# The first block's projection stage in another order: head 0's attention among the convolution's chunks, mean and variance behind the last chunk

## The reference

```python
q, k, v, u = split(proj)                # 4 heads, q and k with two parts of 64, v with 128
q, k = apply_rope(q), apply_rope(k)
a = softmax(q1 k1^T, causal) - lam * softmax(q2 k2^T, causal)
attn = rmsnorm(a @ v) * sub_g * (1 - lam_init)
z = (u_a + b_a) * sigmoid(u_gate + b_gate)          # 512 channels, as 4 chunks of 128
z = depthwise causal convolution, 31 taps, + bias
conv = silu(layer_norm(z over channels))
h = h + concat(attn, conv) @ w_out
h = h + (silu(gate) * up) @ w_down                  # gate, up = rmsnorm(h) @ w_gate_up
```

## Time and profile before

| | us |
|---|---|
| median of 3 runs (1738.6 to 1741.92) | 1740.06 |
| the profiled execution | 1738.21 |
| its span, first to last instruction | 1736.6 |
| TensorE busy in the span | 1661.4 (96%) |
| VectorE busy | 971.8 (56%) |
| ScalarE busy | 688.5 (40%) |
| GpSimd busy | 62.0 (4%) |

### The profile page before, as it was taken

The page is one execution under the profiler, slowest core; times in us unless marked ns, Lnnn a source line. Parts: engine busy times, 40 slices in busy tenths (PEclk is TensorE's granted clock), DMA queues, the critical chain, the costliest instruction groups (busy, mean ns, idle before and its releaser), DMA issues.

```text
span 1736.6 us, 26907 instructions
## 1 busy us (share of the span) xinstructions
PE 1661.4 (96%) x10642; PEld 1309.8 (75%) x10642; DVE 971.8 (56%) x1705; ACT 688.5 (40%) x1225; POOL 62.0 (4%) x48
## 2 busy tenths in 40 slices
PE   8889999998989999999999999999999999999997
PEld 6678999986789999878898989897544454545453
DVE  6967777769677777576756697665121212121212
ACT  2155434321554444465543577632222232323222
POOL 0100000001000000005110000000000000000000
PEclk9999999999999999999999999998999999999999
DMA  6222666752226667532402333336899999999993
GB/s 278 97 74 101 228 230 242 262 198 97 95 100 219 236 242 290 200 122 96 141 25 98 146 132 135 142 139 269 327 423 422 421 422 422 422 422 422 423 422 137
DMA packets 63963, 404.66 MB, mean 233 GB/s; under 512 B 12928, under 2 KB 14464, under 8 KB 15232
## 3 DMA queue, kind: packets, MB, share of 16 engines
q1 hardware_dynamic: 63440, 401.86, 59.3%
q10 hardware_dynamic: 432, 1.51, 0.2%
HBM read 401.91 MB, written 1.44 MB: 232 GB/s over the span
## 4 chain that ended last, share of the span: by engine, by line
PE 76%; DVE 16%; ACT 5%; issue 1%; DMA 0%; SPq 0%; DVEq 0%; ACTq 0%
PE ps L1441 20%; PE ps L847 19%; PE ps L988 10%; DVE big L2234 5%; PE ps L1414 4%; PE ps L1431 4%; PE ps L672 2%; DVE inv L2487 2%; DVE wlo L2298 2%; ACT whi L1634 2%; PE ps L1321 1%; DVE wlo L2665 1%; PE ps L1353 1%; PE ps L1382 1%; ACT wb L1842 1%
## 5 line engine op out<-in xcount | busy, mean ns | idle before, releaser
L2298 DVE TENSOR_TENSOR wlo<-ring,whi 128x2048 fp32r<-128x2048 f32 x76 | 174.2, 2292 | 90.3 <-ACT whi L1634 90.0
L847 PE MATMUL ps<-hg_hi,whi 128*128 128x272 f32 (+1 forms) x672 | 191.3, 285 | 2.4 <-DVE big L2430 2.4
L847 PE MATMUL ps<-hg_hi,wlo 128*128 128x272 f32 (+1 forms) x672 | 191.4, 285 | 0.0
L847 PE MATMUL ps<-hn_lo,whi 128*128 128x272 f32 (+1 forms) x672 | 190.8, 284 | 0.0
L1441 PE MATMUL ps<-big 128*64 128x512 f32 x816 | 181.8, 594 | 0.7 <-ACT big L2122 0.7
L1441 PE MATMUL ps<-ring,big 128*64 128x512 f32 x816 | 181.7, 594 | 0.0
L1634 ACT ACTIVATE whi<-ring 128x2048 fp32r<-128x2048 f32 x76 | 144.9, 1907 | 70.4 <-PE ps L847 51.8
L2951 DVE TENSOR_TENSOR ylo<-ps,yhi 128x512 fp32r<-128x512 f32 x68 | 47.0, 692 | 172.2 <-ACT yhi L2145 137.3
L672 PE MATMUL ps<-hn,ring 128*128 128x272 f32 x576 | 138.3, 398 | 0.0
L1441 PEld LDWEIGHTS ps<-big 128*64 128x64 f32 x816 | 57.5, 137 | 106.9 <-issue 106.6
L1441 PEld LDWEIGHTS ps<-ring,big 128*64 128x64 f32 x816 | 57.1, 137 | 107.2 <-issue 106.8
(11 more groups left out here) (456 smaller groups left out, 3585.9 us busy)
## 6 DMA issues: line engine op xcount, KB each, us to landing
ring<-in_stream SPq DMA_DIRECT2D x277, 1024.0 KB, 5.4
big<-in_stream SPq DMA_DIRECT2D x102, 1024.0 KB, 10.6
h<-in_xT SPq DMA_DIRECT2D x1, 1088.0 KB, 5.1
out_xT<-h SPq DMA_DIRECT2D x1, 1024.0 KB, 4.7
big<-in_consts ACTq DMA_DIRECT2D x1, 896.0 KB, 4.7
cst<-in_consts SPq DMA_DIRECT2D x1, 576.0 KB, 6.1
cs<-in_c_rows SPq DMA_DIRECT2D x1, 512.0 KB, 17.6
big<-in_consts ACTq DMA_DIRECT2D x1, 326.5 KB, 3.5
```

The source lines that it names most:

```text
L847: m = mm(out, a[:, at_:at_ + P], b[:, kept], start=first and i == 0, stop=last and i == 2)
L2298: v.tensor_tensor(wlo[j][:, :], ring[:, j, :], whi[d % 3][:, :], ALU.subtract).then_inc(wlo_ready, 1)
```

## The change

The first slot is now `qk0`, so the raw product gives q0 and k0 and the pair of VectorE evictions goes into `raw`. Head 0 (units 0 and 1) is rotated, scored and weighed among the convolution's chunks; the taps are spread over a longer list of other VectorE work; `mu` and `var` move from behind k2 and q3 to behind V3. The tail's `weigh` waits for all values. `DC + 2` counts of `raw_step` become `DC`. Lines of the order before, which stand in the kernel above, are cut.

```diff
-IN_ORDER = "glu0 glu1 glu2 glu3 qk0 v01 qk1 qk2 qk3 v23".split()
+IN_ORDER = "qk0 glu0 glu1 v01 glu2 glu3 qk1 qk2 qk3 v23".split()
-WORK = "v0 g0 v1 g1 v2 g2 v3 g3 q0 k0 rq0 V0 rk0 V1 t0 q1 t1 k1 rq1 q2 rk1 k2 mu rq2 q3 var rk2 k3 rq3 V2 rk3 s0 s1 V3 t2 t3".split()
+WORK = ("q0 k0 v0 rq0 g0 rk0 v1 g1 V0 V1 t0 t1 v2 g2 v3 g3 q1 k1 rq1 q2 rk1 k2 rq2 q3 rk2 k3 rq3 V2 rk3 s1 V3 mu "
+        "s0 var t2 t3").split()
@@ TensorE @@
-                        if slot_name == "glu1" and n == 0:
+                        if slot_name == "glu0" and n == 0:
                             W(pe, "hn_ready", k + 1, l)
...
-                    bank = ps[:, BANK[("v0", "g0")[n]], :]
+                    bank = ps[:, BANK[("q0", "k0")[n]], :]
...
                         if UNITS[u] == "tail":
+                            W(pe, "v_ready", 8, l)
...
+                chunk("glu0", 0, "v0")
+                rotate("q0")
+                chunk("glu0", 1, "g0")
+                rotate("k0")
+                chunk("glu1", 0, "v1")
+                scores(0)
+                chunk("glu1", 1, "g1")
+                scores(1)
+                chunk("v01", 0, "V0")
+                turn_probs(0)
+                chunk("v01", 1, "V1")
+                turn_v(0)
+                turn_probs(1)
+                turn_v(1)
+                chunk("glu2", 0, "v2")
+                weigh(0)
+                chunk("glu2", 1, "g2")
+                weigh(1)
                 chunk("glu3", 0, "v3")
                 chunk("glu3", 1, "g3")
...
                 chunk("qk1", 0, "q1")
                 chunk("qk1", 1, "k1")
                 rotate("q1")
                 chunk("qk2", 0, "q2")
                 rotate("k1")
                 chunk("qk2", 1, "k2")
+                scores(2)
+                rotate("q2")
+                chunk("qk3", 0, "q3")
+                scores(3)
+                rotate("k2")
+                turn_probs(2)
+                chunk("qk3", 1, "k3")
+                turn_probs(3)
+                weigh(2)
+                rotate("q3")
+                scores(4)
+                chunk("v23", 0, "V2")
+                weigh(3)
+                rotate("k3")
+                scores(5)
+                turn_probs(4)
+                chunk("v23", 1, "V3")
+                tail_scores()
+                turn_v(2)
+                turn_probs(5)
+                weigh(4)
                 W(pe, "conv_ready", 1, l)
                 bank = take("mu")
...
+                scores(7)
+                weigh(5)
+                turn_probs(6)
+                turn_v(3)
+                scores(8)
                 W(pe, "ln_step", 3, l)
                 bank = take("var")
...
                 weigh(6)
                 turn_probs(7)
+                weigh(7)
+                turn_probs(8)
...
                 add_out(0, conv_part, True, False, [0])
-                weigh(7)
-                turn_probs(8)
                 weigh(8)
@@ ScalarE @@
+                gate_out(0)
+                gate_out(1)
+                exps(0)
                 value_out(0)
+                exps(1)
+                probs_out(0)
                 value_out(1)
                 turned_value_out(0)
+                probs_out(1)
+                turned_value_out(1)
+                head_out(0)
+                gate_out(2)
+                head_out(1)
+                gate_out(3)
                 raw_out("q1")
                 raw_out("k1")
                 raw_out("q2")
                 raw_out("k2")
                 exps(2)
...
+                exps(4)
+                value_out(2)
+                head_out(3)
+                exps(5)
+                probs_out(4)
+                high_weights(0)
+                value_out(3)
+                exps(6)
+                turned_value_out(2)
+                probs_out(5)
+                head_out(4)
+                exps(7)
+                W(act, "ln_step", 2, l)
+                f(lsq[:, :, :], xc[:, :, :], ACT.Square).then_inc(ln_step, 1)
+                head_out(5)
+                probs_out(6)
+                turned_value_out(3)
+                exps(8)
                 W(act, "ln_step", 4, l)
                 f(root[:, 1, :], work("var", L), ACT.Sqrt, bias=small[:, 60:61], scale=1.0 / (CC * P)).then_inc(ln_step, 1)
+                head_out(6)
+                probs_out(7)
+                head_out(7)
...
+                probs_out(8)
+                W(act, "conv_out", CC, l)
+                f(xhi[:, 4:8, kept], cat[:, 4:8, kept], ACT.Copy).then_inc(xhi_ready, 1)
+                head_out(8)
+                high_weights(1)
+                W(act, "o_squared", 10, l)
+                f(small[:, 49:58], small[:, 40:49], ACT.Sqrt, scale=1.0 / P).then_inc(o_squared, 1)
                 if l == 0:
                     act.wait_ge(ada_loaded, 16)
                     f(cs[:, :], cs[:, :], ACT.Silu).then_inc(cs_ready, 1)
@@ VectorE @@
-                    if c == 0:
-                        dve.wait_ge(slot_done, l * PE_SLOTS + 1)
-                        v.tensor_tensor(sgl[:, 0, :], ps[:, BANK["g0"], 0:L], inv[:, 0, :], ALU.mult).then_inc(raw_step, 1)
-                        v.tensor_tensor(xc[:, 0, :], ps[:, BANK["v0"], 0:L], inv[:, 0, :], ALU.mult).then_inc(raw_step, 1)
...
+                for name in ("q0", "k0"):
...
+                    v.tensor_tensor(raw[:, j, :], ps[:, BANK[name], 0:L], inv[:, 0, :], ALU.mult).then_inc(raw_ready, 1)
                 W(dve, "lam_step", 3, l)
...
+                with_sin("q0")
+                with_sin("k0")
+                glu(0)
+                convolve(8, (0,))
+                maxima(0)
+                convolve(4, (0,))
                 glu(1)
+                difference(0)
+                maxima(1)
+                convolve(8, (0, 1))
+                difference(1)
+                convolve(26, (0, 1))
                 glu(2)
+                convolve(18, (0, 1, 2))
                 glu(3)
                 convolve(12, (0, 1, 2, 3))
+                with_sin("q1")
+                convolve(6, (0, 1, 2, 3))
+                with_sin("k1")
+                convolve(4, (0, 1, 2, 3))
+                maxima(2)
+                with_sin("q2")
+                difference(2)
+                maxima(3)
+                convolve(4, (0, 1, 2, 3))
+                with_sin("k2")
+                difference(3)
+                convolve(6, (0, 1, 2, 3))
+                with_sin("q3")
+                maxima(4)
                 convolve(8, (0, 1, 2, 3))
+                difference(4)
+                with_sin("k3")
+                maxima(5)
+                convolve(8, (0, 1, 2, 3))
+                difference(5)
                 convolve(sum(TAPS - t for t in taps.values()), (0, 1, 2, 3))
+                maxima(6)
+                maxima(7)
+                difference(6)
                 W(dve, "ln_step", 1, l)
...
+                difference(7)
+                maxima(8)
+                low_weights(0)
                 W(dve, "ln_step", 5, l)
                 link(v.reciprocal(inv[:, 1, :], root[:, 1, :]))
...
+                difference(8)
                 W(dve, "xhi_ready", 1, l)
...
+                low_weights(1)
                 W(dve, "o_squared", 11, l)
                 link(v.reciprocal(small[:, 49:58], small[:, 49:58]))
```

More of the change, by code:

```diff
@@ L810, in _ @@
                 m.then_inc(ln_step, 1)
[L811 to L827, removed]
-                weigh(4)
-                scores(7)
-                turn_v(3)
-                weigh(5)
-                turn_probs(6)
-                scores(8)
                 weigh(6)
                 turn_probs(7)
+                weigh(7)
+                turn_probs(8)
                 def both_parts(d):
@@ L1634, in high_weights @@
                     f(whi[d % 3][:, :], ring[:, s % RING, :], ACT.Copy).then_inc(whi_ready, 1)
-                for c in range(3):
-                    gate_out(c)
-                gate_out(3)
-                raw_out("q0")
-                raw_out("k0")
+                gate_out(0)
+                gate_out(1)
+                exps(0)
                 value_out(0)
+                exps(1)
+                probs_out(0)
                 value_out(1)
                 turned_value_out(0)
-                exps(0)
+                probs_out(1)
[4 more added lines that the diff above has]
+                gate_out(3)
                 raw_out("q1")
-                turned_value_out(1)
-                exps(1)
                 raw_out("k1")
-                probs_out(0)
                 raw_out("q2")
-                probs_out(1)
-                head_out(0)
                 raw_out("k2")
-                W(act, "ln_step", 2, l)
-                f(lsq[:, :, :], xc[:, :, :], ACT.Square).then_inc(ln_step, 1)
                 exps(2)
-                head_out(1)
                 raw_out("q3")
@@ L1661, in _ @@
                 probs_out(2)
+                raw_out("k3")
+                probs_out(3)
+                head_out(2)
+                exps(4)
```

(35 more changed lines are left out.)

75 lines of the change are left out of this document (9 added, 66 removed).

## The result

The changed kernel takes **1768.15 us** (median of four: 1764.17, 1767.8, 1768.51, 1768.8) against 1739.67 of the kernel before (four runs): a ratio of 1.0159, 95% interval 1.0143 to 1.0175. It is slower by 28 us; 1761 in 1750 to 1770 was forecast. The profiled execution is the quickest of the four: 1764.17, a span of 1762.5, 25.9 longer than before's.

What follows compares the result with a forecast made beforehand. TensorE was taken as bound, with some 17 us idle per layer to win, and VectorE's taps as the reason for lateness. Layer 0's +8.7 and 1.4 and layer 1's +11.0 gave +21: 1759 profiled, 1761 median, range 1750 to 1770.

Steps and rivals of the forecast that it cites:

- C + 34: First finish matmul in layer 0: 34 us behind the last convolution tap (C), after a chain of queued steps.
- Part 1: Head of the stage: VectorE waits 2.8 and 2.7 us, chunk v1 stalls 2.2, taps start at 31.3, not 24.0.
- rival (d): Exposed table loads pay the skill page's drain, three ScalarE steps each 1.4 us later: +8, 1769 us; chance 0.02.
- Parts 2 and 3: Middle through last tap: 76.5 us VectorE work from 21.0 plus 14.6 of waits; last tap at 112, 22 later.
- rival (a): Faster, removed stalls kept: needs VectorE's waits ahead of the last tap under 6 us in layer 0; chance 0.07.
- Part 4: Last tap to first finish matmul: TensorE idles 8.4 us ahead of weigh(4); the exposed chain takes 34 us.
- the sum: Both layers: +8.7 and 1.4 us in layer 0, +11.0 in layer 1; together +21, so 1759 profiled, 1761 median.
- Rival (c): Slower, but by half: the tail keeps the full clock, +12 us, 1752 us; chance 0.2.

Runs made afterwards that it cites:

- The two halves: New head of stage with mean and variance placed as before: 1754.73 us; kernel before with only mean and variance put late: 1766.65 us.
- both moves: Changed kernel with ScalarE's turned value and turned probabilities ahead of exps(6), and output-weight roundings moved off the chain's end: 1744.71 us (10 runs).
- the sized fill: Changed kernel, turned value and roundings moved, gaps filled with fewer unread matmuls (8, 5, 2 in place of 15, 6, 4): 1739.39 us, ratio 0.9994.

## Why the prediction was right, and where it was off

**Direction, mechanism and places** were right. Taps start at 32.58 against 31.3, chunk v1 waits 2.09 against 2.2, the one wait ahead of weigh(4) is 7.66 against 8.4, and waits of 2.84, 3.20 and 3.77 stand ahead of turn_probs(8), the first product and the finish, where 3 to 4 each was written. From the last tap to the finish it takes 33.9 us (114.59 to 148.46), against C + 34, and not by luck: the steps in between are where they were put (exps(8) over 15.2 behind the last tap against 15.0, the layer norm's product 20.2 against 20.0, `cat_lo` 24.9 against 25.0).

**Part 1.** VectorE's two waits are 1.95 and 2.68, against 2.8 and 2.7. The first is shorter because two of lambda's three small steps take 0.66 and 0.68 us beside GpSimd's multiplication instead of 0.16. That multiplication was itself mis-sized: the 4.4 us of its first operation, taken from the 5.31 of two, are not its price but that place's; two take 1.47 us here. Neither moved the sum, since TensorE ends both waits. The rule of the Trainium skill (ScalarE: Activation LUTs, What ACT_TABLE_LOAD costs), 1.38 us of drain on top of a load, does not show in this trace either; load and next ACTIVATE at two exposed places on ScalarE:

```profile
30.23 1.28 ACT L1581 ACT_TABLE_LOAD   x1 [11.87 <-PE ps L673]
31.52 0.49 ACT L1581 ACTIVATE big<-ps,par 128x272 f32<-128x272 f32 x1
...
43.39 1.28 ACT L1607 ACT_TABLE_LOAD   x1
44.68 0.37 ACT L1607 ACTIVATE big<-ps,small 128x128 f32<-128x128 f32 x1
```

That is 1.29 us from start to start, as the 1.30 of the earlier trace rows; rival (d) falls.

**Parts 2 and 3.** Of the waits up to the last tap, five are within 0.2 of what was written (glu(0), gate 1, exps(0), maxima(2), maxima(3): 0.48, 1.55, 1.69, 1.83, 2.68). One more is off: maxima(0) waits 2.45, not 0.6, for scores(0) behind chunk v1, and v1 takes 5.59 us at the lower clock. All eight waits sum to 15.3 us against 14.6; rival (a) needed less than 6. The last tap ends at 114.6, 2.6 late: 1.35 of the start and 1.3, net, of this. In layer 1 v1 takes 3.90, and the last tap is over 90.8 us behind the first chunk (91.1 was forecast).

**Part 4 and the sum.** The term that was mis-sized is the lower clock, and with it most of the 7 us that are missing. The prediction priced it at 2.2 us at the mean and 1.5 at the first product, 1.4 more behind layer 0's finish, and nothing at chunk v1 or in layer 1's finish. The trace has 1.8 at v1, of which 1.3 reach the last tap, 2.45 behind layer 0's finish and 1.95 behind layer 1's (1.3 just behind the finish, the rest in the second block). Rival (c), full clock in the tail, did not come about. With the gaps filled the changed kernel takes 1750.9 where (c) has 1752, but that the numbers meet is in part chance: (c) takes 9 us off the forecast, the fill took 17 off the median. The profiled execution comes out at 1764.17 against 1759 forecast: 1.35 of the start, 1.05 and 1.95 behind the finishes, and 0.5 within the stages (1.2 more in layer 0, 0.7 less in layer 1). The remaining 4 us are between the profiled execution and the median of the four, and they were put at 1.85, the distance in the kernel before, which had no reason to carry over.

**What was wrong in the reading of the kernel before** is a step that the sum happened not to use: "all that the change can win is the some 17 us of idle time per layer", with 5.5 + 2.3 us for the gap ahead of scores(0). The filled gap in the kernel before shows that closing it or its low clock is worth nothing by itself, because VectorE's taps, not TensorE, set when the mean starts. It was worth something where work from behind the mean was put into it, in the kernel with the mean behind k3. The two halves run alone show that the sum over layers of "later taps" and "later mean" holds only along one chain: 15 and 27 us alone, 28 together.

## What to carry to other kernels

Find the one operation at which two engines meet (here the mean over the channels, which needs the last tap of VectorE and a free place on TensorE), and ask of every idle gap whether it lies ahead of that point on the engine that is late there. A gap on the other engine is worth nothing by itself (1740.29 with it filled); it is worth what can be moved into it from behind the meeting point (8 us more of TensorE's work ahead of the mean, 12 us less in all). Work that is moved ahead of it on the late engine is paid in full, and everything queued behind it in program order, on ScalarE too, should be either independent and placed ahead, or really dependent on it. Count for each new wait the possible loss of clock behind it as well: here 7.66 us were followed by 3.83 for 2.00, and 2.1 us by 5.59 for 3.83 in one layer and by 3.90 in the other.

## What the runs showed of the hardware

**The time of one kernel follows its granted clock.** Ten executions of the kernel with both moves lie between 1742.78 and 1752.15 us; those with a mean granted clock of 0.983 to 0.985 took 1742.8 to 1745.6, the three with 0.980 took 1750.1 to 1752.2 (one at 0.982: 1748.6). The kernel before, at 0.983 to 0.986, lies between 1738.48 and 1741.16 in the same comparison. The changed kernel's profiled execution had 0.976, its three others 0.973, and these are the 4 us above. The rows show that the lower level does not fall on the same work each time: with the roundings moved and the same waits ahead, layer 0's scores(8) rows take 0.60 us as in the changed kernel, and layer 1's take 1.06:

```profile
486.39 0.80 PE L696 MATMUL ps<-cst,big 128*128 128x128 f32 x3 [0.92 <-DVE big L2361]
486.99 1.06 PE L710 MATMUL ps<-big 128*128 128x256 f32 x2
```

So a single profile of a kernel with many gaps gives its clock term only to some microseconds. Nor do such differences stay in the stage. From the reciprocal of the norm behind layer 1's finish to the end all these kernels run the same program. Their profiled executions take from 1214.4 us (the sized fill) to 1220.4 (the mean behind k3) for it, the kernel before 1217.9. A single profiled execution is thus no measure of a change of a few microseconds here. What decides where the clock falls was not settled.

**A small operation's price depends on its neighbour.** VectorE's one-column steps of lambda take 0.66 and 0.68 us while GpSimd multiplies (22.96 to 24.4) and 0.16 behind it; in the kernel with the mean behind k3, where GpSimd is idle then, all three take 0.15 to 0.16:

```profile
23.07 0.66 DVE L2315 TENSOR_TENSOR small<-small 128x1 f32<-128x1 f32 x1
23.77 0.68 DVE L2316 TENSOR_TENSOR small<-small,par 128x1 f32<-128x1 f32 x1
24.48 0.16 DVE L2317 TENSOR_TENSOR small<-par 128x1 f32<-128x1 f32 x1
```

Larger operations show the same: the 6 taps from 94.06 on, beside GpSimd's product at 94.65, take 3.06 us or 0.51 each, and the 26 from 51.17 on, with GpSimd idle, 10.80 or 0.42. No run here took GpSimd's operation away at these places, so that it is the cause is argued, not shown.
